# A long convolution's opening: the signal's outer tiles placed among the filter's stages, and the next group's filter weights requested early

## What is computed

```
def fft_long_conv(u, h, bias):
    L = u.shape[1]
    n = 2 * L
    uf = jnp.fft.rfft(u, n=n, axis=1)
    hf = jnp.fft.rfft(h, n=n, axis=0)
    y = jnp.fft.irfft(uf * hf[None], n=n, axis=1)[:, L // 2: L // 2 + L]
    return y + u * bias

    ...
    filt = (hdn @ f32(w3)).reshape(L, HYENA_ORDER, D_HYENA)
    ...
    filt = filt * jnp.exp(-offset[:, None, None] * rates)
    return filt * lax.rsqrt(jnp.sum(filt * filt, axis=0, keepdims=True) + RMS_EPS)
    ...
    z = x1 * fft_long_conv(v, filt[:, 0], fb[0])
    y = x2 * fft_long_conv(z, filt[:, 1], fb[1])
    return y * jax.nn.silu(zh.astype(jnp.float32))
```

## Time and profile before

| | |
|---|---|
| median of 3 runs | 1684.63 us (1683.03 to 1684.9) |
| profiled execution, its own time | 1683.12 us |
| its span, first to last instruction | 1681.3 us |
| mean granted TensorE clock | 0.978 of full |
| TensorE busy | 1581.0 us, 94% of the span |
| VectorE, ACT, POOL busy | 710.3, 673.7, 307.6 us |

### The profile page before, as it was taken

How to read it: one execution, slowest core, us unless ns; L and a number is a source line. 1 busy time by engine, 2 the same in 40 slices (tenths; PEclk the granted TensorE clock), 3 DMA queues, 4 the chain that set the end, 5 groups by cost and what they waited for, 6 DMA issues and landing times. The chain is left out here.

```text
span 1681.3 us, 23549 instructions
## 1 busy us (share of the span) xinstructions
PE 1581.0 (94%) x8886; PEld 1358.3 (81%) x8886; DVE 710.3 (42%) x1123; ACT 673.7 (40%) x1371; POOL 307.6 (18%) x297
## 2 busy tenths in 40 slices
PE   7799999999999999999997799999998556999997
PEld 3788888888888888888886789999897556888886
DVE  1654420333333333010201677777675256555553
ACT  2885212342222222131111655565653256555451
POOL 1551000000000000000000021212122005665652
PEclk9899999999999999999998899999999789999999
DMA  9241521222221122121113644535353564665651
GB/s 363 75 129 50 207 76 55 75 72 75 75 74 69 75 75 95 49 100 49 47 50 147 176 123 119 166 92 169 93 145 76 169 210 157 193 206 181 202 189 51
DMA packets 128191, 201.72 MB, mean 120 GB/s; under 512 B 12555, under 2 KB 75713, under 8 KB 121190
## 3 DMA queue, kind: packets, MB, share of 16 engines
q1 hardware_dynamic: 128102, 200.52, 37.8%
HBM read 122.45 MB, written 52.86 MB: 104 GB/s over the span
## 5 line engine op out<-in xcount | busy, mean ns | idle before, releaser
L454 PE MATMUL bank<-h_hi,w_hi 128*128 128x512 f32 (+1 forms) x840 | 325.1, 387 | 0.0
L456 PE MATMUL bank<-h_hi,w_lo 128*128 128x512 f32 (+1 forms) x840 | 323.4, 385 | 0.0
L455 PE MATMUL bank<-h_lo,w_hi 128*128 128x512 f32 (+1 forms) x840 | 323.2, 385 | 0.0
L454 PEld LDWEIGHTS bank<-h_hi,w_hi 128*128 128x128 f32 x840 | 158.5, 189 | 31.2 <-issue 0.2
L456 PEld LDWEIGHTS bank<-h_hi,w_lo 128*128 128x128 f32 x840 | 158.5, 189 | 31.3
L455 PEld LDWEIGHTS bank<-h_lo,w_hi 128*128 128x128 f32 x840 | 158.7, 189 | 30.9 <-issue 0.2
L454 PE MATMUL bank<-w_hi,h_hi 128*128 128x512 f32 (+1 forms) x448 | 164.5, 367 | 0.0
L455 PE MATMUL bank<-w_lo,h_hi 128*128 128x512 f32 (+1 forms) x448 | 164.1, 366 | 0.0
L456 PE MATMUL bank<-w_hi,h_lo 128*128 128x512 f32 (+1 forms) x448 | 164.1, 366 | 0.0
L822 DVE SCALAR_TENSOR_TENSOR work<-work,coef 128x504 f32<-128x504 f32 (+1 forms) x84 | 62.3, 742 | 239.8 <-ACT work L610 239.7
L600 ACT ACTIVATE work<-bank 128x512 f32<-128x512 f32 (+1 forms) x72 | 40.4, 562 | 299.2 <-PE bank L456 299.1
(11 more groups left out here) (225 smaller groups left out, 2845.4 us busy)
## 6 DMA issues: line engine op xcount, KB each, us to landing
H<-spectrum SPq DMA_DIRECT2D x192, 128.0 KB, 2.4
stage<-in_w_in SPq DMA_DIRECT2D x18, 1024.0 KB, 5.9
s_hy<-work SPq DMA_DIRECT2D x48, 256.0 KB, 2.2
xin<-s_hy SPq DMA_DIRECT2D x8, 1024.0 KB, 5.2
kq<-s_k SPq DMA_DIRECT2D x32, 256.0 KB, 4.6
v<-s_v SPq DMA_DIRECT2D x32, 256.0 KB, 5.0
mb<-s_rows SPq DMA_DIRECT2D x32, 256.0 KB, 5.6
late<-in_x SPq DMA_DIRECT2D x16, 512.0 KB, 4.8
```

Of the source, the lines that this page charges most:

```text
L454: pe.matmul(out, lhs[0], rhs[0], start=(k == 0), stop=False)
L455: pe.matmul(out, lhs[0], rhs[1], start=False, stop=False)
L456: return pe.matmul(out, lhs[1], rhs[0], start=False, stop=(k == KD - 1))
```

## The change

The signal's first unit of group 0 is taken apart. Its x_outer tiles go right behind the prologue's turn tiles, x_rows behind the first norm, and the next turn tiles between the second norm and f_rows. `unit` leaves these stages out for g = 0, o = 0. ACT and VectorE evict in the same new order. Since `B` now holds signal tiles, the second square is written to `A2f`. The list `OPENING` replaces `PROLOGUE` and includes group 0. `load_group` is split: `load_third` (w3 and window) and `load_bias`. The second group's `load_third` is issued by SyncE in the prologue, once w3_lo is made and the last in_time tiles are evicted; its bias stays where it was. TensorE and ACT wait for the constants set by POOL later than before.

```
+def opening_tiles():
+
+    tiles = in_time_tiles("P") + signal_tiles("P", "turn") + signal_tiles(0, "x_outer") + [("P", "norm", 0)]
+    tiles += signal_tiles(0, "x_rows") + filter_outer_tiles("P") + [("P", "norm", 1)] + signal_tiles(0, "turn")
+    tiles += filter_rows_tiles("P") + inner_pairs("P", None)
+    return tiles + unit_body(0, True) + unit_tiles(1, True)
...
-            def load_group(g):
+            def load_third(g):
                 sp.dma_start(w3[:, :], d["fw3"][g]).then_inc(group_in, 16)
                 sp.dma_start(window[:, :, :], d["window"][g]).then_inc(group_in, 16)
+
+            def load_bias(g):
                 sp.dma_start(fb[P // 2:P // 2 + 1, :, :], d["fbias"][g]).then_inc(group_in, 16)
...
+            sp.wait_ge(w3_low, 1)
+            for t in (W_TILES - 2, W_TILES - 1):
+                wait_taken(sp, 0, ("P", "in_time", t))
+            load_third(1)
             wait_filled(sp, 0, ("P", "turn", F_TILES - 1))
             load_x(GROUPS)
             load_gates(0)
...
                     wait_count(sp, f_ready, g, 2, 2)
-                    load_group(g + 1)
+                    if not (isinstance(g, int) and g == 0):
+                        load_third(g + 1)
+                    load_bias(g + 1)
...
+            turn_x(0, "P")
+            outer_signal(0, 0)
+            pe.wait_ge(const_set, 2)
+            norm(0, "P", 0, 0)
+            signal_rows(0, 0)
+            pe.wait_ge(f_ready, 1)
+            for t in range(S_TILES):
+                outer_tile(0, ("P", "f_outer", t), f[:, 0], t)
+            norm(0, "P", 1, 1)
+            turn_next(0, 0)
+            filter_rows(0, "P")
...
             high_w3(0, 1)
+            take_turned(0, "P", nat)
+            square(0, "P", 0, in_Bf)
+            take_outer(0, 0, "x_outer", B, 2)
+            square(0, "P", 1, in_A2f)
             act.wait_ge(const_set, 2)
-            square(0, "P", 0, Bf)
-            take_turned(0, "P", nat)
-            square(0, "P", 1, B)
             root(0, "P", 0)
+            take_signal_rows(0, 0)
             take_outer(0, "P", "f_outer", Bf, 1)
             root(0, "P", 1)
+            take_turned(0, 0, x1)
             take_filter_rows(0, "P")
...
             take_turned(0, "P", nat)
-            sum_squares(0, 0, Bf)
+            take_outer(0, 0, "x_outer", B, (1, 3))
+            sum_squares(0, 0, in_Bf)
+            take_outer(0, 0, "x_outer", B, (5, 7))
             invert(0, "P", 0)
+            take_signal_rows(0, 0)
             scale(0, 0, 0)
-            sum_squares(0, 1, B)
+            sum_squares(0, 1, in_A2f)
+            take_turned(0, 0, x1)
             invert(0, "P", 1)
             scale(0, 1, 1)
```

More of the change, by code:

```diff
@@ L1703, in filter_rows_tiles, with signal_tiles, unit_head, unit_body @@
     return [(u, "f_rows", t) for t in range(Q_TILES)]
[L1706 to L1716, removed]
+def signal_tiles(o, stage):
+    return [(o, stage, t) for t in range({"x_outer": S_TILES, "turn": F_TILES, "x_rows": Q_TILES}[stage])]
+def unit_head(o, more):
+    return signal_tiles(o, "x_outer") + (signal_tiles(o, "turn") if more else []) + signal_tiles(o, "x_rows")
+def unit_body(o, ahead):
+    more, tiles = ahead or o == 0, []
     if more:
@@ L2011, in inner_tile @@
                 mm.then_inc(summed, 1)
[L2013 to L2024, removed]
-            filter_rows(0, "P")
-            pe.wait_ge(filter_in, 16)
-            for t in range(Q_TILES):
-                inner_tile(0, "P", "f_inner", "f_rows", A2f, t)
-            pe.wait_ge(const_in, 32)
             def inverse(g, o, t):
@@ L2056, in unit @@
                     to_rows(g, (o, "x_rows", t), B, t)
+            pe.wait_ge(layer_lo, 2)
+            pe.wait_ge(w3_low, 1)
+            in_time(0, "P")
+            pe.wait_ge(start_in, 32)
+            pe.wait_ge(x_in, 16)
+            turn_x(0, "P")
[9 more added lines that the diff above has]
+            filter_rows(0, "P")
+            pe.wait_ge(filter_in, 16)
+            for t in range(Q_TILES):
+                inner_tile(0, "P", "f_inner", "f_rows", A2f, t)
+            pe.wait_ge(const_in, 32)
+            def unit(g, o, ahead):
+                more = ahead or o == 0
+                if not (isinstance(g, int) and g == 0 and o == 0):
+                    outer_signal(g, o)
+                    if more:
+                        turn_next(g, o)
+                    signal_rows(g, o)
                 if more:
@@ L2174, in unit @@
                 more = ahead or o == 0
-                take_outer(g, o, "x_outer", B, 2)
-                if more:
-                    take_turned(g, o, nat if o else x1)
-                for t in range(0, Q_TILES, 2):
-                    take(g, (o, "x_rows", t), A2[:, 4 * t:4 * t + 4])
+                if not (isinstance(g, int) and g == 0 and o == 0):
+                    take_outer(g, o, "x_outer", B, 2)
+                    if more:
+                        take_turned(g, o, nat if o else x1)
+                    take_signal_rows(g, o)
                 if more:
@@ L2210, in take, with take_outer @@
                 dve.tensor_copy(dst, src).then_inc(taken["dve"], 1)
-            def take_outer(g, u, stage, dst):
-                for t in range(1, S_TILES, 2):
+            def take_outer(g, u, stage, dst, tiles=range(1, S_TILES, 2)):
+                for t in tiles:
                     src = by_k1[wait_filled(dve, g, (u, stage, t))]
@@ L2219, in take_turned, with take_signal_rows @@
                     take(g, (u, "turn", t), dst[:, 4 * t:4 * t + 4])
+            def take_signal_rows(g, o):
+                for t in range(1, Q_TILES, 2):
+                    take(g, (o, "x_rows", t), A2[:, 4 * t:4 * t + 4])
             def low_w3(g, loads):
@@ L2288, in unit @@
                 more = ahead or o == 0
-                take_outer(g, o, "x_outer", B)
-                if more:
-                    take_turned(g, o, nat if o else x1)
-                for t in range(1, Q_TILES, 2):
-                    take(g, (o, "x_rows", t), A2[:, 4 * t:4 * t + 4])
+                if not (isinstance(g, int) and g == 0 and o == 0):
+                    take_outer(g, o, "x_outer", B)
+                    if more:
+                        take_turned(g, o, nat if o else x1)
+                    take_signal_rows(g, o)
                 for t in range(Q_TILES):
```

70 lines of the change are left out of this document (38 added, 32 removed).

## The result

| | before | after |
|---|---|---|
| median, lowest to highest | 1683.83 us (1682.12 to 1687.33, 8 runs) | 1694.45 us (1686.32 to 1700.16, 8 runs) |
| profiled execution, its span | 1683.12, 1681.3 | 1686.32, 1684.5 |

The ratio is 1.0053, 95% interval [1.0037, 1.007]: slower by about 9 us (10.6 between the medians), and outside the range. Among the executions of the kernel after, the mean granted clock lies between 0.980 in a fast one and 0.973 in the slowest. They also spread over 14 us, where those of the kernel before spread over 5. The profiled execution is one of the two fastest, so this trace alone doesn't show the usual loss. It has to be read for what could go wrong in it.

The account below looks back on a forecast made before the run. TensorE was taken as the bound, so the start of the second group's in-time tiles prices everything: 974.2 − 975.7 = −1.5 us, which against the median of 1684.6 gives 1683.1 us. Range 1680.4 to 1687.6.

Parts of the forecast that it names:

- Steps 1 to 4: Opening, up to the filter's spread into H: f_outer +5.1 us, then −1.2, so the spread starts 3.9 later.
- Step 5: Spread into H: DMA keeps it 16.2 us long, products wait for H and end at 972.1 instead of 975.2.
- the rival of a faster spread: Spread into H: if faster once it starts later, products start 5.8 us earlier, total 1678.9; chance 0.10.
- Step 6: Second group's loads: w_hi waits for the bias, landing at 973.3; in-time tiles at 974.2, 1.3 us later than products allow.
- the clock falls in the new gaps: TensorE at half clock in x_rows and f_outer: +5.0 us, so +3.5 in all, 1688.1; chance 0.12.
- It falls only once: TensorE's clock falls at f_outer or before the in-time tiles: +2.1 us, so +0.6, 1685.2; chance 0.18.
- The sum at full clock: Start of the second group's in-time tiles: 974.2 against 975.7, −1.5 us; chance 0.43.

Follow-up runs that it names:

- two_queues: The change with half of the filter's first spread (12 of 24 transfers) issued from ACT's queue: 1684.32 us, ratio 0.9999.
- bias_apart: The change with the bias on its own semaphore, so w_hi no longer waits for it: 1687.71 us, ratio 1.0017.
- best: The change with bias on its own semaphore, GpSimd's multiply behind w_lo, filter scaled first, and half the spread from ACT's queue: 1681.42 us, ratio 0.9976.
- all_three: The change with bias on its own semaphore, GpSimd's multiply behind w_lo in the first group, and filter scaled first: 1682.76 us, ratio 0.999.
- after_again: The changed kernel once more, unaltered: 1693.04 us, ratio 1.0039.
- gate_waits: The change with GpSimd's multiply of the first group made to wait for w_lo, the bias still awaited: 1687.70 us, ratio 1.0021.
- scale_first: The change with VectorE scaling the first filter before it takes the signal's row tiles: 1689.83 us, ratio 1.0026.
- gate_first: bias_apart with w_lo made to wait for GpSimd's multiply in the first group: 1695.33 us, ratio 1.0059.
- moves_only: The change's moved tiles, with w3 and window of the second group requested where they were before: 1692.55 us, ratio 1.0049.
- warm_after: The change with 40 idle matmuls in TensorE's gaps: 1693.02 us, ratio 1.0057.
- warm_gates: warm_after with GpSimd's multiply of the first group made to wait for w_lo: 1693.77 us, ratio 1.0052.
- warm kernel before: The kernel before with 37 idle matmuls in its first two gaps, run twice: 1689.14 us (ratio 1.0026) and 1691.78 us (1.0034).

## Why the prediction was wrong

- **Steps 1 to 4 held.** f_outer +16.61 after the turn tiles against 16.92; in front of the root the table load, with no gap behind it (932.28 + 1.28, root 933.58), so charging 1.28 and no more was right. f_outer 5.47 long; the spread 28.27 after the turn tiles against 28.5.
- **Step 5 held in the change** (products 2.6 apart, waiting 0.46 to 1.07 for H). A second queue shortened the way from the spread's start to w_lo by 0.2 us (two_queues against bias_apart) and 1.1 (best against all_three), so the spread is bound by DMA for the most part, and the rival of a faster spread fell.
- **Step 6 found the mechanism and stopped short.** It says that w_hi waits for the bias and that the in-time tiles are "1.3 later than the products would allow". Measured: 1.27. But the prediction costed this only as a delay of TensorE. It never asked what else starts 1.3 us after the last product. GpSimd's sum takes 1.26 to 1.28, and its multiply of 4.6 us comes right behind. The trace of before has both, and no row of GpSimd stands in the prediction. This step failed. It makes w_lo and the multiply start within 0.02 to 0.14 us of each other in the two profiles of the change, and a lost race costs 4.3 us on VectorE (4.69 against 0.42). Its share of the loss is 5.3 to 6.8 us by the medians (after_again and the first measurement against gate_waits), 3.0 to 5.4 by the ratios. In the openings of the profiles it is 4.4 (from the first spread to the third 80.2 in scale_first, 75.7 in gate_waits). That the change usually loses the race is inferred from these medians and not seen: w_lo was ahead in both of its profiles.
- **The rival "the clock falls in the new gaps" had the right price and too small a chance.** It got 0.12 for both early stages slow. In the ten profiles of the change and its variants without idle matmuls, both were slow in three (after_again, bias_apart, two_queues), one in three (gate_waits, gate_first, all_three), and none in four (after, moves_only, scale_first, best). The forecast price was +5.0 up to f_outer's end; counted from the turn tiles, after_again has f_outer 2.5 later than the first profile and 1.7 longer, together 4.2. What failed is "None is clearly longer than what brought it down": each gap was weighed alone, by its length.
- **The third gap, before the in-time tiles, was the usual one.** The clock fell in it, or just behind it, in seven of the ten profiles: after, after_again, moves_only, scale_first and gate_first (3.1 to 7.7 us long), gate_waits (3.27) and bias_apart (1.91). It stayed up in two_queues (1.55), all_three (1.91) and best (0.76). From the start of these tiles to the third spread it is 52.3 us where the clock stays up, and 53.8 to 54.9 where it falls, so a fall costs 1.5 to 2.6. In the first profile this alone took back the 2.4 us gained by then, which is the rival "It falls only once".
- **The sum at full clock was near.** Without falls the opening is 2.4 and 2.1 us shorter than before (warm_after, warm_gates), against the −1.5 forecast. Beside the warm kernel before this is −0.4 and +0.15: in the opening, moving the tiles is worth almost nothing beyond what it does to the clock.

What stays open: with the race taken out, the change is still 2.7 us above the kernel before (1687.70 against 1684.97). One profile of gate_waits has its opening 2.2 late, with f_outer at half clock for most of its length (8.40 long) and part of the in-time tiles, which would account for it; how often this happens was not counted, since only one execution per kernel is profiled.

A rival for this rest was not tested. From the eighth spread to the end, the kernels without moved tiles and without idle matmuls take 420.8 to 421.3 us in three profiles, the change 424.2 and 427.6, and its variants 420.0 (bias_apart) to 427.6 (best). So nine of the ten profiles with moved tiles are 1 to 7 us longer in a part where nothing was changed. Of the 12.8 us by which the profile of after_again exceeds that of before, 6.7 lie there. The fastest kernel has this too, so it does not explain why the change is slower than its variants. But it may be a price of the moves, for instance of where the code lies, or chance; these runs don't decide it.

## What to carry to other kernels

A wait of 1.3 us in front of a 0.4 us instruction is not worth 1.3 us: look at what every other engine starts in that time, GpSimd above all if it reads SBUF while VectorE reads two inputs from there. Make the order of two such instructions certain, by a semaphore or by a wait on what is really needed (the bias row was not). A gap moved into the middle of a busy stretch can cost again in clock: here 1.5 to 3.0 us for each stage that it slowed. And where one trace of a kernel shows two instructions within 0.1 us of each other that can hold each other up, another execution may have them the other way round. How far the executions spread is no proof of such a race: those of all_three and best, where it is excluded, still spread over 10 and 11 us.

## What the runs showed that I had not expected

- A two-input VectorE instruction of 0.42 us took 4.69 when it started 0.09 us after a GpSimd multiply; 0.02 us ahead of it, it took 0.42, and the multiply 4.82 instead of 4.50 to 4.61.
- The clock fell in a gap of 2.7 us that had a norm's two matmul records in its midst (after_again, 934.0), and stayed up in the same gap in another execution of the same kernel (after). The Trainium skill, TensorE: Matmul & The Clock Gate, "The HAM clock gate", has the monitor run freely beside the program; the two traces agree.
- 37 or 40 more matmuls in the opening cost 5 to 9 us, with "issue" waits of TensorE, some 200 us later, at the loop's second round.
